# One slot for gathered rows left empty while rows 98 to 126 are asked for

## What is computed

```python
h2 = _rmsnorm(x, norm2_g)
q = (h2 @ w_q)                                   # 8 heads
s = einsum('thcd,hcnd->thcn', q, keys)           # scores against 2 x 128 keys
...                                              # top 16 of the 16 x 16 sums: idx, best_s
gate = softmax(best_s)
u = take(u_tab, idx)                             # a row of 2048 for each token, head, place
act = gelu(einsum('thkd,td->thk', u, h2))
out = einsum('thk,thkd->td', gate * act, take(v_tab, idx))
```

## Time and profile before

| | us |
|---|---|
| median of 3 runs | 4244.01 (4230.96 to 4246.35) |
| the profiled execution, its own time | 4246.9 |
| its span | 4245.1 |
| busy: TensorE / VectorE / ScalarE / GpSimd | 3601.6 / 2898.7 / 912.6 / 1242.7 |
| gathers L757, 272 of them, GpSimd busy | 643.5, mean 2.366 |
| share of the 16 DMA engines: gathers q0 / weights q1 | 53.8% / 30.7% |

### The profile page before, as it was taken

How to read it: one execution, slowest core, us unless ns; L and a number is a source line. 1 busy time by engine, 2 the same in 40 slices (tenths; PEclk the granted TensorE clock), 3 DMA queues, 4 the chain that set the end, 5 groups by cost and what they waited for, 6 DMA issues and landing times. The chain is left out here.

```text
span 4245.1 us, 40919 instructions
## 1 busy us (share of the span) xinstructions
PE 3601.6 (85%) x14174; PEld 2363.2 (56%) x14174; DVE 2898.7 (68%) x4311; ACT 912.6 (21%) x2041; POOL 1242.7 (29%) x772
## 2 busy tenths in 40 slices
PE   8999999999999999868589999789999777555555
PEld 6777789446766667655578886353444334211111
DVE  6455568102989999973867667784665888766666
ACT  2232210101222211132211221111111233233222
POOL 1000000000233332231223333142232555666665
PEclk9999999999999999989799999899999999999999
DMA  3111158888999999999999999999999999999998
GB/s 126 60 60 70 50 209 301 300 316 299 386 392 397 389 420 406 412 376 404 405 403 426 419 424 425 423 402 427 426 427 374 416 416 400 407 418 418 418 417 361
DMA packets 162505, 1488.54 MB, mean 351 GB/s; under 512 B 24512, under 2 KB 24640, under 8 KB 33344
## 3 DMA queue, kind: packets, MB, share of 16 engines
q0 software_dynamic: 81408, 948.08, 53.8%
q1 hardware_dynamic: 70704, 512.44, 30.7%
q10 hardware_dynamic: 10256, 26.35, 1.6%
HBM read 1465.82 MB, written 20.97 MB: 350 GB/s over the span
## 5 line engine op out<-in xcount | busy, mean ns | idle before, releaser
L757 POOL DMA_INDIRECT arena_c<-in_peer_uv,arena_c x272 | 643.5, 2366 | 2571.3 <-DVE arena_o L1563 1532.0
L1877 PE MATMUL bank<-arena_h,wring 128*128 128x128 f32 (+4 forms) x6272 | 1193.7, 354 | 65.7 <-DMA wring<-in_w_in 28.2
L1550 DVE SCALAR_TENSOR_TENSOR arena_c<-arena_c 128x2048 f32<-128x2048 f32 (+1 forms) x512 | 916.0, 1789 | 320.6 <-DMA arena_c<-in_peer_uv_rest,arena_c 256.6
L1877 PEld LDWEIGHTS bank<-arena_h,wring 128*128 128x128 f32 x6272 | 957.3, 197 | 300.3 <-DMA wring<-in_w_in 27.3
L1563 DVE SCALAR_TENSOR_TENSOR arena_o<-arena_c,arena_o 128x2048 f32<-128x2048 f32 (+1 forms) x511 | 945.2, 1850 | 210.1 <-ACT arena_c L935 172.9
L2316 PE MATMUL bank<-arena_c,cols 128*128 128x512 f32 x960 | 508.9, 658 | 356.7 <-ACT cols L1123 356.7
L2316 PEld LDWEIGHTS bank<-arena_c,cols 128*128 128x128 f32 x960 | 177.2, 203 | 664.6 <-ACT cols L1123 531.9
L2287 PE MATMUL bank<-wring,arena_h 128*128 128x512 f32 x1024 | 445.9, 595 | 16.3 <-DMA wring<-in_peer_u_tiles 16.3
L768 POOL DMA_INDIRECT cols<-dots,cols x240 | 340.5, 1419 | 133.3 <-issue 122.7
L929 ACT ACTIVATE arena_c<-arena_c 128x1 f32<-128x1 f32 x272 | 55.1, 203 | 1388.1 <-DVE arena_c L1550 1375.5
L2287 PEld LDWEIGHTS bank<-wring,arena_h 128*128 128x128 f32 x1024 | 192.8, 190 | 268.1 <-issue 231.6
(11 more groups left out here) (261 smaller groups left out, 3182.8 us busy)
## 6 DMA issues: line engine op xcount, KB each, us to landing
wring<-in_w_in SPq DMA_DIRECT2D x176, 1024.0 KB, 11.1
wring<-in_peer_u_tiles SPq DMA_DIRECT2D x64, 1024.0 KB, 18.1
wring<-in_w_out SPq DMA_DIRECT2D x48, 1024.0 KB, 10.4
wring<-in_peer_w_q SPq DMA_DIRECT2D x48, 1024.0 KB, 10.0
wring<-in_gla_w_o SPq DMA_DIRECT2D x32, 1024.0 KB, 12.0
wring<-in_conv_w_pw SPq DMA_DIRECT2D x32, 1024.0 KB, 16.5
wring<-in_w_v SPq DMA_DIRECT2D x16, 1024.0 KB, 4.8
wring<-in_w_ga SPq DMA_DIRECT2D x16, 1024.0 KB, 4.8
```

The lines of the kernel that those rows point to most:

```text
L757: pool.indirect_dma_start(out=slot_of(n), out_offset=None, in_=uv_tab, in_offset=column(idx_cur, U % 2, k)).then_inc(landed(n)[0], 16)
L1550: V.scalar_tensor_tensor(row, row, 1.0, block_of(h2, n // P)[:, first:], ALU.mult, ALU.mult, accum_out=act_u[:, n % TOP:n % TOP + 1]).then ...
L1877: last = M(ps[bank][:, at:at + hi - lo], w_tile(slot)[:, k, :], act_in[:, k, lo:hi], start=k == 0, stop=k == KT - 1)
```

## The change

`FEWER_ROWS` is `range(PW_AT - 1, 2 * TOP * PH // 2 - 1)`, which is 98 to 126. For these rows GpSimd waits for one more addition, that of row n - 3, before it asks for row n. Rows below 98 and from 127 on are asked for as before. No instruction is added, removed or moved on any engine: 29 waits have a value greater by one.

```diff
+FEWER_ROWS = range(PW_AT - 1, 2 * TOP * PH // 2 - 1)
...
                 for k in range(TOP):
                     n = U * TOP + k
 
-                    pool.wait_ge(row_used, n + 1)
+
+                    pool.wait_ge(row_used, n + 1 + (n in FEWER_ROWS))
                     if n in BEHIND_HEAD:
                         pool.wait_ge(s_ev, 2 * (BEHIND_HEAD[n] + 1))
                     pool.indirect_dma_start(out=slot_of(n), out_offset=None, in_=uv_tab,
```

## The result

The changed kernel takes 4251.25 us (median of 20 runs, 4243.34 to 4258.25) against 4243.54 us before (20 runs, 4230.96 to 4256.25): a ratio of 1.0019, with an interval of 1.0012 to 1.0027, or **7.7 us slower**; the interval stands for some 5 to 11 us. The forecast was 7 us slower. One run of a later experiment, of rows 119 to 126, took 4957.38 us at a granted TensorE clock of 0.74, where all others have 0.96, and is left out of that kernel's time.

What follows compares the result with a forecast made beforehand. DMA bytes were taken as the bound around the rows in question, with TensorE full behind them. 0 + 7.0 + 0 = +7.0 us on the median of 4244.0 gave 4251 us, range 4239 to 4267.

Steps and rivals of the forecast that it cites:

- The row lag: Steps 115 to 131: the queue lags one row, 2.1 MB, so dots 118 to 130 come about 7.0 us later.
- Part one: Steps 98 to 114: each row lands when its successor landed, still before its dot; cost and gain 0.
- The thin cover at step 113: Row 114's old landing came 0.25 us before dot 113; a miss there would cost a microsecond or two.
- The pace: Rows 119 to 131: rows keep coming every 7.38 us with two under way in place of three.
- Who waits for step 130: At step 130 TensorE waits 3.38 us for ScalarE's query copy, so the merge stage opens late, at 2159.4.
- The first rival, absorption: Query heads or merge stage: TensorE's own weights come last, or the stage gives time back; 4244 us, chance 0.14.
- The third rival, the weights: w_pw2 and w_out stages: fewer rows let weights through earlier, up to 22.8 us gained; 4221 us, chance 0.08.
- The reset: Around 2188 to 2190 us DMA engines run empty, all slots full; the same state returns 7 us later.

Runs made afterwards that it cites:

- the two late runs: Only rows 119 to 126 asked for one addition later, against the kernel before, run twice: 4244.63 us (1.0012) and 4244.08 us (1.0002).

## Why the prediction was right

**The row lag.** Every row took the place of the next, and the loss was that of one row where the steps begin to wait for landings: +7.0 us forecast, 34.8 us in place of 29.4 (27.6 in the run of the same kernel) between dots 113 and 118, 7.6 us at dot 130, 7.7 us in the median. That forecast and median lie within 1 us of each other is partly luck: the interval of the difference reaches from 5 to 11 us, and the second profile of unchanged instructions puts the lag at the merge nearer 13 us. The run of rows 98 to 118 shows that the lag is taken there once and for all, and the two late runs that an empty slot costs next to nothing once the queue is never without a row.

**Part one, nearly free.** The row's bandwidth at 1843 went to nobody, as forecast, and its successors' transfers kept their times. The thin cover at step 113 did not hold: dot 113 waited 2.56 us in the change and 2.33 with rows 98 to 118, where 0.25 us were to spare. Stage 98 to 113 took 165.1 and 164.9 us in these two, above all six profiles that leave it alone (160.4 to 163.4); in the change with the copies moved, where dot 113 did not wait, it took 162.8. So this term was put at 0 and is about 2 us in two profiles of three; the range held "a microsecond or two" for it. Dot 130 comes 288.8 and 288.2 us behind dot 98 where dot 113 waits and 286.3 where it does not, so it may be paid at dot 130 too; this rests on one profile each. (Dot 114, some 1.3 us behind the landing of row 115, was tighter than dot 101, which the prediction names; nothing follows from it.) That the stage came out so near to neutral rests on where the row goes missing: with the row made up within it (rows 98 to 110) it lost some 5 us or more.

**The pace.** 7.38 us was forecast to stay with two rows under way; it is 88.9 us for 12 steps in both, 7.41. The packets went 721 to 723. The Trainium skill (DMA: Bandwidth & Descriptors, section "Queues, rings and completion order") says that an engine goes round the queues that have work, a packet from each; the trace agrees. It shows the limit too: with two slots empty the engines pause, and the pace is 8.09 us. The prediction's remark that the slot count limits the queue at steps 118 to 131 did not hold there: rows 119 to 126 with three slots came at all but the same pace, and what counts is the row that was missing before.

**Who waits for step 130.** ScalarE's copies carry the lag to TensorE: shown by moving them, which takes the lag out of the merge stage's opening (120.8 us from dot 113 in place of 128.8). The first rival, absorption, had something in it that the prediction saw (copies last by only some 3 us): with four slots the weights are as late as the rows, so moving the copies gains nothing there. The third rival, the weights, did not show in the change before the heads, where the missing row left idle time; it did where only rows 111 to 118 were withheld. In the change it was seen in the heads, as TensorE's 14.2 us of waits for tiles went to nothing, and it gave no time back there, since ScalarE was bound to the steps.

**The reset.** The stage from the first merge to dot 207 is 563.0 us after the change and 563.3 before, so the delay went through whole up to there, as forecast. That a row is lost when the DMA engines pause around 2188 with a slot empty is borne out by rows 127 to 207: some 4.8 us, of which 3.0 us are seen at that pause.

## What to carry to other kernels

In this kernel a buffer left empty cost what could have been fetched while the DMA engines were idle, once, and not by its number of steps: look for the last pause of the engines before the stretch where transfers are late. Withheld beside weights that were waited for, it gave them a little time. While the queue kept a request waiting, one buffer fewer shortened the landing and not the pace; the next one fewer let the queue run dry. And before believing that a late operand is hidden, see whose copies stand behind it on an in-order engine.

## What was not expected of the hardware

With two slots a pace of 7.7 us a row or a little more was expected, and 8.09 came; how it comes about was seen only in the trace: 373 GB/s in place of 422, in short pauses between slices that are as full as before. And profiled executions differ by 3 us in one stage alone where nothing in it was changed (160.4 to 163.4 from dot 98 to 113), so effects of this size are only read from stages and from many runs.
